# Moving the last RWKV head pair's finish into the block of the sparse attention's projection

## The reference

```python
h_p = rmsnorm(y_p, norm_mix[layer]) @ w_in_even[li]
# nsa_project: columns 0 to 1303
q = rope(rmsnorm(q, qn), pos); k = rope(rmsnorm(kv[:, :, :, 0], kn[:, None, :]), pos)
gates = jax.nn.sigmoid(h[..., NSA_Q + NSA_KVW:NSA_IN])
# rwkv_mix, after the scan over the tokens
mean = jnp.mean(y, axis=-1, keepdims=True)
var = jnp.mean(jnp.square(y - mean), axis=-1, keepdims=True)
y = ((y - mean) * lax.rsqrt(var + RWKV_GN_EPS)).reshape(B, T, W) * ln_w + ln_b
y = y + (jnp.sum(r * k * r_k, axis=-1, keepdims=True) * v).reshape(B, T, W)
return y * g, S, p[:, -1]
```

## Time and profile before

| | us |
|---|---|
| three timed runs | 4452.33, 4461.98, 4477.48 (median 4461.98) |
| the profiled execution, its own time | 4452.25 |
| its span in the trace | 4450.4 |
| the finish block, the store of `rw_last` and the wait for the weights | 892.6 to 936.6 of the span |
| the projection's nine tiles | 936.6 to about 1110 |

### The profile page before, as it was taken

One profiled execution on the slowest core, in us unless ns is written; L12 is line 12 of the kernel. 1 busy time (PEld: TensorE's weight loads), 2 busy tenths in 40 slices (PEclk: granted clock), 3 DMA queues, 4 the chain that ended last, 5 costly groups with the idle time before them and its releaser, 6 DMA issues. The chain is left out here.

```text
span 4450.4 us, 62608 instructions
## 1 busy us (share of the span) xinstructions
PE 3873.8 (87%) x26171; PEld 3226.1 (72%) x26171; DVE 1361.1 (31%) x2514; ACT 795.4 (18%) x1483; POOL 481.8 (11%) x342
## 2 busy tenths in 40 slices
PE   6698988869778856869999999999996869999996
PEld 4467767734445633859999998576675859999996
DVE  2344534422256622232112123223223132112211
ACT  1122220101045600121111111112111121111110
POOL 0000000000400000112122221000000112222221
PEclk9799998889879965989999999999995989999998
DMA  2000000010400021111111110201112111111112
GB/s 86 13 11 16 21 6 11 7 71 20 112 24 1 6 75 46 58 36 49 40 41 52 38 43 31 93 15 59 40 40 86 63 39 51 39 42 47 39 42 91
DMA packets 75722, 189.10 MB, mean 42 GB/s; under 512 B 30836, under 2 KB 45108, under 8 KB 72260
## 3 DMA queue, kind: packets, MB, share of 16 engines
q1 hardware_dynamic: 62724, 157.97, 10.8%
q0 software_dynamic: 8448, 27.27, 1.9%
q10 hardware_dynamic: 4352, 1.05, 0.2%
HBM read 161.34 MB, written 29.04 MB: 43 GB/s over the span
## 5 line engine op out<-in xcount | busy, mean ns | idle before, releaser
L392 DVE TENSOR_TENSOR ff_prod<-ff_silu,ps 128x384 f32<-128x384 f32 x132 | 62.4, 528 | 874.0 <-PE ps L234 874.0
L234 PE MATMUL ps<-ffn_high,ff_gh 128*128 128x384 f32 (+1 forms) x1056 | 234.7, 330 | 71.9 <-POOL ff_gl L276 71.9
L2323 PE MATMUL ps<-act,gl_w 128*128 128x384 f32 (+1 forms) x768 | 243.3, 477 | 0.0
L234 PE MATMUL ps<-ff_hh,ff_dh 128*128 128x384 f32 (+1 forms) x1056 | 233.2, 328 | 4.6 <-DVE ff_hl L397 4.6
L234 PEld LDWEIGHTS ps<-ffn_high,ff_gh 128*128 128x128 f32 x1056 | 181.9, 189 | 72.9 <-POOL ff_gl L276 72.9
L234 PE MATMUL ps<-ffn_high,ff_gl 128*128 128x384 f32 (+1 forms) x1056 | 234.1, 330 | 0.0
L234 PE MATMUL ps<-ffn_low,ff_gh 128*128 128x384 f32 (+1 forms) x1056 | 234.0, 329 | 0.0
L234 PE MATMUL ps<-ffn_high,ff_ul 128*128 128x384 f32 (+1 forms) x1056 | 232.7, 328 | 0.0
L234 PE MATMUL ps<-ffn_low,ff_uh 128*128 128x384 f32 (+1 forms) x1056 | 232.7, 328 | 0.0
L234 PE MATMUL ps<-ffn_high,ff_uh 128*128 128x384 f32 (+1 forms) x1056 | 232.7, 328 | 0.0
L234 PE MATMUL ps<-ff_hh,ff_dl 128*128 128x384 f32 (+1 forms) x1056 | 232.7, 328 | 0.0
(11 more groups left out here) (562 smaller groups left out, 7069.8 us busy)
## 6 DMA issues: line engine op xcount, KB each, us to landing
ff_wg<-in_wg SPq DMA_DIRECT2D x44, 512.0 KB, 3.6
ff_wu<-in_wu SPq DMA_DIRECT2D x44, 512.0 KB, 3.6
ff_wd<-in_wd POOLq DMA_DIRECT2D x48, 256.0 KB, 3.0
ff_wd<-in_wd POOLq DMA_DIRECT2D x32, 320.0 KB, 3.4
ns_past<-in_cache_slc SPq DMA_DIRECT2D x64, 128.0 KB, 2.0
rw_w<-in_w_rwkv SPq DMA_DIRECT2D x14, 512.0 KB, 3.6
np_w<-in_w_nsa SPq DMA_DIRECT2D x2, 2608.0 KB, 11.8
resid<-in_x SPq DMA_DIRECT2D x1, 4352.0 KB
```

Of the source, the lines that this page charges most:

```text
L234: mm = pe.matmul(g.ps[:, bank + c, 0:n], w[:, k, :], x[:, kx, o:o + n], start=(first and i == 0), stop=(last and i == 2))
L392: m = dve.tensor_tensor(prod[:, o:o + n], silu[:, o:o + n], g.ps[:, 3 + c, 0:n], ALU.mult)
L2323: mm = pe.matmul(out[:, 0:n], w[:, k, :], g.act[:, k, o:o + n], start=(k == 0), stop=(k == KT - 1))
```

## The change

The finish of the last pair and the store of `rw_last` become part of the block of `nsa_project`. The blocks `rwkv_finish` and that of the store are gone, and `rwkv_mix` now returns its buffers; three of them (`rw_lora`, `rw_lw`, `rw_last`) are allocated on the other side of SBUF so that they outlive it. The squares and the root go to `g.resid` (slots 1 and 0) in place of `rw_e` and `rw_cum`. The weights are loaded as eight transfers with a semaphore each, and TensorE waits for each k; the gain has a semaphore of its own, on which VectorE waits.

```diff
-def nsa_project(g, d):
+def nsa_project(g, d, rw):
+    rest = g.resid
+    rw_y, rw_rt, spread = rest[:, 7, :], rest[:, 0, :], rest[:, 1, :]
+    rw_banks = [(g.ps[:, 3 + c, 0:n], o, n) for c, (o, n) in enumerate(CH)]
...
-        w_here = [sem(f"w_here{i}") for i in range(2)]
+        w_here = [sem(f"w_here{i}") for i in range(KT)]
...
         @block.sync
-            for i in range(2):
-                sp.dma_start(w[:, 4 * i:4 * i + 4, :], d.w_nsa[:, 4 * i:4 * i + 4, :]).then_inc(w_here[i], 16)
-            sp.dma_start(gain[:, :], d.qk_gain.partition_broadcast(P)).then_inc(w_here[0], 16)
+            for k in range(KT):
+                sp.dma_start(w[:, k, :], d.w_nsa[:, k, :]).then_inc(w_here[k], 16)
+            sp.dma_start(gain[:, :], d.qk_gain.partition_broadcast(P)).then_inc(gain_here, 16)
+            sp.dma_start(d.last, rw.last[:, :, :]).then_inc(rw_stored, 16)
+            sp.wait_ge(rw_gated, 1)
+            sp.dma_start(d.rwkv_out[:, 3, :], rw_y).then_inc(rw_stored, 16)
...
+            sp.wait_ge(rw_stored, 32)
...
         @block.tensor
+                if t == 1:
+                    pe.wait_ge(rw_gated, 1)
                 for k in range(KT):
                     x = g.act[:, k, t * P:t * P + R]
-                    if t == 0 and k % 4 == 0:
-                        pe.wait_ge(w_here[k // 4], 32 if k == 0 else 16)
+                    if t == 0:
+                        pe.wait_ge(w_here[k], 16)
+                        if k == 3:
+                            pe.wait_ge(rw_centered, 1)
+                            for p, o, n in rw_banks:
+                                mm = pe.matmul(p, g.blk, spread[:, o:o + n], start=True, stop=True)
+                            mm.then_inc(rw_var, 1)
+                        if k == 6:
+                            pe.wait_ge(rw_root, 1)
+                            for p, o, n in rw_banks:
+                                mm = pe.matmul(p, rw.lw[:, 1, 3 * P:4 * P], rw.lora[:, 1, o:o + n], start=True, stop=True)
+                            mm.then_inc(rw_gate, 1)
...
+            for p, o, n in rw_banks:
+                mm = pe.matmul(p, g.blk, rw_y[:, o:o + n], start=True, stop=True)
+            mm.then_inc(rw_mean, 1)
             project(*tiles[0])
...
         @block.scalar
+            act.wait_ge(rw_var, 1)
+            for p, o, n in rw_banks:
+                a = act.activation(rw_rt[:, o:o + n], p, ACT.Sqrt, bias=g.col["gneps"], scale=1.0 / HD)
+            a.then_inc(rw_root, 1)
...
         @block.vector
+            dve.wait_ge(rw_mean, 1)
+            for p, o, n in rw_banks:
+                dve.scalar_tensor_tensor(rw_y[:, o:o + n], p, -1.0 / HD, rw_y[:, o:o + n], ALU.mult, ALU.add)
+            dve.drain()
+            dve.tensor_tensor(spread, rw_y, rw_y, ALU.mult).then_inc(rw_centered, 1)
+            dve.wait_ge(rw_root, 1)
+            dve.reciprocal(rw_rt, rw_rt)
...
+            dve.wait_ge(rw_gate, 1)
+            for p, o, n in rw_banks:
+                m = dve.tensor_tensor(rw_y[:, o:o + n], rw_y[:, o:o + n], p, ALU.mult)
+            m.then_inc(rw_gated, 1)
             for t, R in tiles:
...
                 if t == 0:
-                    dve.wait_ge(w_here[0], 32)
+                    dve.wait_ge(gain_here, 16)
...
-        rwkv_finish(g, d, b, s, 3, y_stored)
-                sp.dma_start(d.last, b.last[:, :, :]).then_inc(small, 16)
-                sp.wait_ge(small, 48)
```

More of the change, by code:

```diff
@@ L490, in _ @@
                     m.then_inc(s.out, 1)
-def nsa_project(g, d):
+def nsa_project(g, d, rw):
     nc = g.nc
+    rest = g.resid
+    rw_y, rw_rt, spread = rest[:, 7, :], rest[:, 0, :], rest[:, 1, :]
+    rw_col = lambda name: g.col[name][:, 3:4]
+    rw_banks = [(g.ps[:, 3 + c, 0:n], o, n) for c, (o, n) in enumerate(CH)]
     tiles = [(t, min(P, TOK - t * P)) for t in range(9)]
@@ L508, in nsa_project @@
         rot = sb("rot", [P, 4, H, 8])
-        w_here = [sem(f"w_here{i}") for i in range(2)]
+        w_here = [sem(f"w_here{i}") for i in range(KT)]
+        gain_here, rw_stored = sem("gain_here"), sem("rw_stored")
+        rw_mean, rw_centered, rw_var, rw_root, rw_gate, rw_gated = (sem("rw_" + n) for n in ("mean", "centered", "var", "root", "gate", "gated"))
         product, squared, summed, root, scaled = sem("product"), sem("squared"), sem("summed"), sem("root"), sem("scaled")
@@ L594, in move @@
                    .then_inc(moved, 1)
+            dve.wait_ge(rw_mean, 1)
[5 more added lines that the diff above has]
+            dve.reciprocal(rw_rt, rw_rt)
+            dve.drain()
+            dve.tensor_tensor(rw_y, rw_y, rw_rt, ALU.mult)
+            dve.drain()
+            dve.tensor_scalar(rw_y, rw_y, rw_col("lnw"), rw_col("lnb"), ALU.mult, ALU.add)
+            dve.drain()
+            dve.tensor_tensor(rw_y, rw_y, rw.bonus[1], ALU.add)
+            dve.drain()
+            dve.wait_ge(rw_gate, 1)
+            for p, o, n in rw_banks:
+                m = dve.tensor_tensor(rw_y[:, o:o + n], rw_y[:, o:o + n], p, ALU.mult)
+            m.then_inc(rw_gated, 1)
             for t, R in tiles:
@@ L1247, with rwkv_mix @@
 RWKV_GROUPS = [(0, 4), (4, 4), (8, 4), (12, 4), (16, 1)]
-def rwkv_mix(g, d):
+def rwkv_mix(g, d, late):
     nc = g.nc
@@ L1253, in rwkv_mix @@
         sb = lambda s, shape: ctx.enter_context(nc.sbuf_tensor("rw_" + s, shape, F32))
+        kept = lambda s, shape: late.enter_context(nc.sbuf_tensor("rw_" + s, shape, F32, side="right"))
         two = lambda s, shape: [sb(f"{s}{i}", shape) for i in range(2)]
@@ L1258, in rwkv_mix @@
             w=[sb("w0", [P, KT, P]), sb("w1", [P, KT, P])],
-            lora=sb("lora", [P, 2, TOK]),
-            lw=sb("lw", [P, 2, 512]),
-            shift=sb("shift", [P, RT, NB]), last=sb("last", [P, RT, 9]),
+            lora=kept("lora", [P, 2, TOK]),
+            lw=kept("lw", [P, 2, 512]),
+            shift=sb("shift", [P, RT, NB]), last=kept("last", [P, RT, 9]),
             r=sb("r", [P, TOK]), k=sb("k", [P, TOK]), cum=sb("cum", [P, TOK]),
@@ L1291, in rwkv_mix @@
         rwkv_heads(g, d, b, h, w_here, st_here, stored, y_stored, filled, taken)
-        rwkv_finish(g, d, b, s, 3, y_stored)
[L1293 to L1297, removed]
-                sp.dma_start(d.last, b.last[:, :, :]).then_inc(small, 16)
-                sp.wait_ge(small, 48)
         g.finished = range(s.product.sem.num, taken[1].num + 1)
+    return b
 RWKV_USES = [0, 1, 2, 3, 4] + [2 + 3 * j + x for j in range(1, 4) for x in (1, 0, 2)]
@@ L2139, in _ @@
                             inverse(*after, level)
[L2142 to L2191, removed]
 def gla_mix(g, d):
@@ L2618, in program @@
                 if layer == 0:
-                    rwkv_mix(m, d)
                     with ExitStack() as nsa:
-                        nsa_layer_buffers(m, nsa)
-                        nsa_project(m, d)
+                        with ExitStack() as late:
+                            rw = rwkv_mix(m, d, late)
+                            nsa_layer_buffers(m, nsa)
+                            nsa_project(m, d, rw)
                         nsa_compress(m, d)
```

## The result

The changed kernel takes 4421.45 us in the median of four runs (4412.39 to 4432.51), the kernel before beside it 4458.48 (4452.33 to 4477.48). The ratio is 0.991, with a 95% interval from 0.9883 to 0.9938: faster by 37 us. A second measurement on another chip, six runs beside eleven of before, gives 4423.04 against 4458.97, ratio 0.9922 (0.9904 to 0.994). The prediction said 4424 and 0.86 for faster.

What follows compares the result with a forecast made beforehand. TensorE, busy 87%, idled 35 us before the projection. Weights' wait 16.25, stores' waits 5.1, slow tile 0 2.9 and 13.6 of ScalarE and VectorE work, less about 0.1, save 37.7: 4461.98 - 37.7 = 4424 us, range 4408 to 4444.

Steps and rivals of the forecast that it cites:

- The start: Merged block's begin: 2.0 us for the heads' last store to land plus 0.4 us, at 892.6 as before.
- The weights: Eight loads of 652 KB: first k lands at 896.55, the rest every 1.6 us, the eighth at 907.7.
- The clock: The mean brings TensorE's clock up, so tile 0 takes 17.1 us in place of 20.0, 2.9 saved.
- The time of one tile: Projection tile on TensorE at the full clock: 17.1 us, or 2.14 us for a k.
- The variance and the gate: TensorE steps placed inside tile 0 of the projection: 2.1 us for the variance, 2.2 for the gate.
- VectorE's chain: From the variance's end to the gated result: 13.66 us as before, gated at 918.8.
- Tile 1's start: Tile 1 of the projection waits 0.9 us for VectorE's gate and starts at 918.9, against 956.6 before.
- What follows the stretch: From tile 1's start on, the change alters nothing; what follows the block's barrier moves as a whole.
- late pieces: Rival: weight pieces land one per 3.95 us or all near 907.3; 30.3 or 27.1 us saved; chance 0.11.
- the one form: Rival's form in which each weight piece pays a lone load's 3.95 us: tile 0 ends at 926.3, 30.3 us saved.
- a clock that stays low: Rival: waits keep TensorE at 1.2 GHz in tile 0, 17 us saved in place of 37.7; chance 0.06.
- the first rival: Weight pieces land late; its lone-load form was priced at 30.3 us saved; chance 0.11.

Runs made afterwards that it cites:

- e5: The changed kernel run again with nothing altered: 4423.04 us, stretch from the mean's first matmul to tile 1's 26.4 us.
- e1: The changed kernel with its weights in two transfers of four k each: 4438.57 us, ratio 0.995 to the kernel before.
- e4: The changed kernel without the finish of the last pair, y stored as it is: 4415.83 us, ratio 0.9896 to the kernel before.
- e9: e1 plus six matmuls that nobody reads between the mean and tile 0: 4423.02 us, ratio 0.9917 to the kernel before.
- e10: The changed kernel with the variance ahead of k = 5 in place of k = 3, one run: stretch from mean to tile 1 30.9 us.
- e6: The changed kernel with the variance ahead of k = 2 in place of k = 3: 4421.56 us, ratio 0.9911 to the kernel before.
- e3: The changed kernel with SyncE waiting for each k's weights to land before issuing the next: 4437.14 us, ratio 0.9946 to the kernel before.

## Why the prediction was right, point by point

The start, 2.4 us after the issue of the heads' last store, is as predicted in every trace that has this store, and the mean takes 3.96 us in every trace that has the mean.

The weights: first k 4.2 us after its issue (predicted 3.95), median 8.0 (8), last 13.1 (12.2). The 13.1 belong to this execution: in the seven other traces with the same eight loads in a row the last took 11.6 to 12.7. TensorE did not wait for it. The 0.20 us of wait for k = 0 are the only cost, and in e5 there is none.

The clock: predicted up from 3.8 us after the mean's start, measured 4.1 us, at the start of tile 0. The earlier trace rows already has it there: a mean of 0.96 over 5.2 us means 0.4 us at 0.50. e1, e4, e9 and e10 show that the term is real: 2.8 us for a pause of 4.97 us in e1, 2.0 for 5.30 us in e10.

The time of one tile was read too short. The prediction took the stretch 956.6 to 973.7 for tile 1 and so 17.1 us for a tile at the full clock. ScalarE takes up tile 0 and tile 1 of the kernel before at

```profile
956.65 0.60 ACT L574 ACTIVATE np_sq<-ps 128x512 f32<-128x512 f32 x1 [53.57 <-PE ps L544]
974.16 0.60 ACT L574 ACTIVATE np_sq<-ps 128x512 f32<-128x512 f32 x1 [15.07 <-PE ps L544]
```

so tile 1 took 17.5 us, a k 2.19 and not 2.14, and the slow start of tile 0 cost 2.5 us and not 2.9. In the changed kernel k = 0 to 2 took 6.67 us where the prediction has 6.4. The variance and the gate took 1.83 us each until the next k where it has 2.1 and 2.2. The two errors cancel: from the start of tile 0 to its end it is 922.57 - 901.14 = 21.43 us, predicted 17.1 + 2.1 + 2.2 = 21.4. That this sum is right to 0.1 us is luck.

VectorE's chain: 923.44 - 909.80 = 13.64 us from the variance's end to the gate's end, predicted 13.66. Neither the tiles in `resid` nor the incoming weights slow it. e10 and e6 show that it is on the path from k = 3 on and off it at k = 2.

Tile 1's start: 26.5 us into the stretch against 26.3 in the sum (918.9 - 892.6); 37.5 us saved against 37.7. The start of tile 0 came 0.16 us later than forecast and k = 0 to 2 took 0.27 us longer; the shorter variance gave 0.1 back.

What follows the stretch: from tile 1's start to the last projection matmul it is 145.3 us, before 145.1, so the projection gives nothing back. For the later stages only whole times can tell. The two profiled executions differ by 18 us outside the stretch. Their mean clocks, 0.905 before and 0.904 after, go the same way but are too near each other to show the cause. The medians of two measurements give 37 and 36 us. That the forecast of 4424 came within 3 us of both medians is in part luck, since single runs of either kernel spread over 20 us and more.

The rivals: late pieces fall by the landings (the first after 4.2 us, the last after 13.1, not all near 14.7 and not one every 3.95) and by e3, which shows what the one form would have cost; a clock that stays low falls by the 1.00 in the stage rows. The price of the first rival was too cheap by 2.6 us: the gate's place behind the wait for k = 6 was left out, and with it the fall of the clock in that wait, which is 1.6 of the 2.6.

## What to carry to other kernels

When a tail of one phase runs on the vector and scalar engines and the head of the next only waits for weights, put both into one block and read the new stretch as a race: here, behind the variance, 13.7 us of ScalarE and VectorE against 12.8 us of matmuls, lost by 0.9 us. Place each step of the tail by where its result must be ready. Look at what shares a semaphore with the first operand: the gain, which nobody needs until tile 0 is done, held TensorE for 7.3 us in the kernel before. Keep TensorE's pauses short, since one of 5 us cost 2 to 3 us beyond its own length, and matmuls that nobody reads gave 2.8 us of it back in the stretch. Where whole times scatter by 20 us, judge edits of a few us by the stretch in the trace.

## What the runs showed of the hardware

Eight transfers of 652 KB issued 0.5 us apart landed at the rate of two of 2,608 KB: in e5 the last landed 11.7 us after its issue at 895.8, which is 15.2 us after the first issue; in e1 the second half landed 14.8 us after its issue at 894.1, also 15.2 us after the first. In the profiled execution of the changed kernel it was 16.7 us. A lone one takes 3.9 us.

In these traces the granted clock follows TensorE's activity late in both directions. In e1, after a mean of 4 us at 1.2 GHz, it was up for the first part of TensorE's wait, fell within the wait, and came back only when tile 0 had run for 5.4 us:

```profile
893.80:897.70 3.90, 3.90 (x6) 1.79 (x6) 0.00 (x0) 0.00 (x0) 0.00 (x0) 0.50 0.82 273
897.70:902.70 5.00, 0.04 (x1) 0.00 (x0) 2.71 (x4) 0.00 (x0) 0.00 (x0) 0.84 1.03 442
902.70:912.10 9.40, 9.39 (x19) 4.69 (x20) 0.00 (x0) 0.00 (x0) 0.00 (x0) 0.71 0.66 275
```

In stretches of half a us it is 1.00 from 898.0 to 901.0, 0.50 from 901.5 to 908.0 and 1.00 from 908.5 on. In e3 four pauses of 1.28 to 1.48 us between the k did not bring it down (1.00 in the stretches of one us around them). It fell within the pause of 2.58 us, shortly before the gate's product at 920.02, and was up again at about 923.1. In e10 it fell within the pause of 5.30 us, at about 918.7, and was up again at 925.5.
